# Moving the norm's inverse root from VectorE to Pool in the projections of two layers

## What is computed

```python
def rms_norm_2(x, w):
    xf = x.astype(jnp.float32)
    y = xf * lax.rsqrt(jnp.mean(xf * xf, axis=-1, keepdims=True) + EPS)
    return (y * w.astype(jnp.float32)).astype(x.dtype)

def even_layer(...):                      # layer 2
    proj = rms_norm_2(x, norm_w) @ w_in   # 2048 x 10272
    ...                                   # short convolutions, SSD scan, memory attention, gates
    return x + concat(y_a, y_b, y_m) @ w_out

def odd_layer(...):                       # layer 3
    proj = rms_norm_2(x, norm_w) @ w_in   # 2048 x 3904
    ...                                   # latent attention, memory attention, gates
    return x + concat(y_c, y_m) @ w_out
```

## Time and profile before

| | us |
|---|---|
| median of 3 runs | 1797.61 (1795.02 to 1800.67) |
| the profiled execution | 1793.41 |
| its span in the trace | 1791.2 |
| TensorE busy | 1742.6 (97%) |
| VectorE busy | 1288.3 (72%) |
| ScalarE busy | 899.7 (50%) |
| Pool busy | 125.9 (7%) |

### The profile page before, as it was taken

How to read it: one execution, slowest core, us unless ns; L and a number is a source line. 1 busy time by engine, 2 the same in 40 slices (tenths; PEclk the granted TensorE clock), 3 DMA queues, 4 the chain that set the end, 5 groups by cost and what they waited for, 6 DMA issues and landing times.

```text
span 1791.2 us, 24344 instructions
## 1 busy us (share of the span) xinstructions
PE 1742.6 (97%) x9671; PEld 1496.0 (84%) x9671; DVE 1288.3 (72%) x1622; ACT 899.7 (50%) x1161; POOL 125.9 (7%) x151
## 2 busy tenths in 40 slices
PE   7989999999999999999999999899999999999997
PEld 6778888877888888888888888788888888888885
DVE  6889979785677756887676777965554766778644
ACT  6444443444466445665444556654444545566532
POOL 3321101000010100110000000000000000000000
PEclk9989999999999999999999999999999999999998
DMA  9979979774445566666544555555565564444552
GB/s 359 385 270 349 343 233 326 230 237 136 146 147 175 188 177 188 189 186 178 165 142 141 155 162 166 167 188 188 188 184 176 161 204 141 141 130 131 176 187 96
DMA packets 310400, 350.70 MB, mean 196 GB/s; under 512 B 11296, under 2 KB 284832, under 8 KB 310288
## 3 DMA queue, kind: packets, MB, share of 16 engines
q1 hardware_dynamic: 295728, 296.24, 53.8%
q0 software_dynamic: 14560, 52.89, 8.2%
HBM read 347.00 MB, written 2.10 MB: 195 GB/s over the span
## 4 chain that ended last, share of the span: by engine, by line
PE 67%; DVE 18%; ACT 6%; issue 5%; DMA 2%; SPq 0%; ACTq 0%; DVEq 0%
PE psG L492 37%; PE psG L493 19%; DVE w_lo L422 6%; ACT w_hi L418 3%; DMA raw<-in_mem_w 2%; PE psG L486 2%; PE psG L488 2%; PE psG L487 2%; DVE ada_sum L1260 1%; DVE P L1218 1%; DVE P L1213 1%; PE psH L1876 1%; DMA ada_ring<-in_w_ada 1%; PE psH L1862 1%; DVE gate_sum L1260 1%
## 5 line engine op out<-in xcount | busy, mean ns | idle before, releaser
L492 PE MATMUL psG<-xA,w_hi 128*128 128x512 f32 x2624 | 942.2, 402 | 4.2 <-DVE w_lo L422 3.7
L422 DVE TENSOR_TENSOR w_lo<-raw,w_hi 128x1024 fp32r<-128x1024 f32 (+1 forms) x560 | 688.5, 1240 | 245.5 <-ACT w_hi L418 244.0
L493 PE MATMUL psG<-xA,w_lo 128*128 128x256 f32 x2624 | 734.5, 280 | 0.0
L418 ACT ACTIVATE w_hi<-raw 128x1024 fp32r<-128x1024 f32 (+1 forms) x560 | 570.4, 1043 | 234.9 <-PE psG L493 167.3
L492 PEld LDWEIGHTS psG<-xA,w_hi 128*128 128x128 f32 x2624 | 492.4, 188 | 123.1 <-issue 10.5
L493 PEld LDWEIGHTS psG<-xA,w_lo 128*128 128x128 f32 x2624 | 495.5, 189 | 4.2 <-issue 3.4
L492 PE MATMUL psG<-yP,w_hi 128*128 128x512 f32 x960 | 337.2, 396 | 3.1 <-DVE P L1218 1.6
L493 PE MATMUL psG<-yP,w_lo 128*128 128x256 f32 x960 | 267.9, 279 | 0.0
L492 PEld LDWEIGHTS psG<-yP,w_hi 128*128 128x128 f32 x960 | 180.0, 187 | 45.9 <-DVE P L1218 1.9
L461 ACT ACTIVATE P<-psG 128x512 f32<-128x512 f32 (+2 forms) x103 | 60.9, 592 | 241.3 <-PE psG L493 241.0
L493 PEld LDWEIGHTS psG<-yP,w_lo 128*128 128x128 f32 x960 | 181.0, 189 | 0.2
(11 more groups left out here) (325 smaller groups left out, 1789.9 us busy)
## 6 DMA issues: line engine op xcount, KB each, us to landing
raw<-in_w_in SPq DMA_DIRECT2D x360, 512.0 KB, 3.8
raw<-in_w_out SPq DMA_DIRECT2D x128, 512.0 KB, 3.4
ada_ring<-in_w_ada POOLq DMA_DIRECT2D x96, 512.0 KB, 6.3
raw<-in_mem_w SPq DMA_DIRECT2D x32, 512.0 KB, 10.1
raw<-in_w_uq SPq DMA_DIRECT2D x24, 384.0 KB, 3.3
raw<-in_w_ukv SPq DMA_DIRECT2D x32, 128.0 KB, 2.4
raw<-in_w_ukv SPq DMA_DIRECT2D x16, 256.0 KB, 3.3
P<-in_memT SPq DMA_DIRECT2D x4, 512.0 KB, 7.1
```

What stands on the lines that cost most here:

```text
L418: nc.scalar.activation(high(n), low(n, raw), ACT.Copy).then_inc(hi_ready, 1)
L422: nc.vector.tensor_tensor(low(n), low(n, raw), high(n), ALU.subtract).then_inc(lo_ready, 1)
L492: nc.tensor.matmul(psG[:, bank + f, :], hi[:, w], x, start=first, stop=False)
L493: last = nc.tensor.matmul(psG[:, bank + f, S:2 * S], lo[:, w], x[:, 0:S], start=False, stop=end)
```

## The change

For every copied product of layers 2 and 3 except the one with a bias (G_DT), VectorE stops after the addition and signals `added`. Pool waits for it, multiplies the same tile by the same root in place, and signals `pool_landed`, for which the users of those blocks now wait. 58 blocks are moved: X0, SZ0, SZ1, M, CZ, CV, CC, CB with four each and X1 with eight; C1, M1 with four each, C2 and KR with one each and the two ZC with eight together. Pool takes them in program order; beside the convolution steps it takes one block before each L629 and one after it. Three of the semaphores of the G_DT step are merged into one to make room, with the same order of waits.

```diff
+        self.by_pool = self.copied and norm in (2, 3) and bias is None
...
         def landed(eng, g, blocks=None):
-            eng.wait_ge(scalar_landed if g.by_scalar else vector_landed,
+            eng.wait_ge(scalar_landed if g.by_scalar else pool_landed if g.by_pool else vector_landed,
                         g.landed0 + (g.blocks if blocks is None else blocks))
...
+            def times_root(g, blocks):
+
+                pool.wait_ge(*((q["nm_rs"], 5) if g in G_ZC else (q["nm_rs"], g.norm + 1)))
+                root = (moved_root if g in G_ZC else norm_root_of(g.norm))[0:g.rows].unsqueeze(1).broadcast_to([g.rows, g.parts, S])
+                for b in blocks:
+                    out = g.dst(b)
+                    pool.wait_ge(added, g.landed0 + b + 1)
+                    nc.gpsimd.tensor_tensor(out, out, root, ALU.mult).then_inc(pool_landed, 1)
...
             add_squares(2)
+            times_root(G_X0, range(4))
             for i in range(6):
+                beside, first = (G_X1, 2 * i) if i < 4 else (G_SZ0, 2 * i - 8)
+                times_root(beside, [first])
                 pool.wait_ge(q["cv_s"], i + 1)
                 nc.gpsimd.tensor_tensor(tiles(i * 4 + XS, 4), tiles(CONV_ACC, 4), tiles(CONV_E, 4), ALU.mult)\
                   .then_inc(q["cv_done"], 1)
+                times_root(beside, [first + 1])
+            for g in (G_SZ1, G_M, G_CZ, G_CV, G_CC, G_CB):
+                times_root(g, range(4))
             landed(pool, G_CB)
...
+            for g in (G_C1, G_C2, G_KR, G_M1, *G_ZC):
+                times_root(g, range(g.blocks))
             add_squares(4)
...
                     ins = v.tensor_tensor(out, product(g, b, 1), out, ALU.add)
+                    if g.by_pool:
+                        ins.then_inc(added, 1)
+                        return
                     if g.norm is not None:
```

## The result

| | before | after |
|---|---|---|
| median, us | 1798.24 (1792.65 to 1803.14, 10 runs) | 1811.7 (1805.37 to 1820.96, 10 runs) |
| the profiled execution | 1793.41 | 1812.53 |
| span in the trace | 1791.2 | 1810.7 |

The ratio is 1.0084, with a 95% interval of 1.0063 to 1.0105: the change makes the kernel 0.84% slower, 13.5 us between the medians. The forecast was 1807.9 us within 1799 to 1815. In the changed kernel the high and low matmuls are L495 and L496, the splits L421 (ScalarE) and L425 (VectorE), the copy L464, the addition L1233, Pool's product L611, and the mask product of the SSD step L1576 with its matmul L2086.

A forecast was written before the change was run, and what follows sets the result against it. TensorE, busy for nearly all of 640 to 1663 us, was taken as the bound. Terms of +4.7 + 4.0 + 1.4 + 0.4 + 0.1 - 0.5 + 0.2 = +10.3 gave 1803.7 us profiled, 1807.9 median, range 1799 to 1815.

The forecast's parts named there:

- The mechanism: Behind additions, a Pool product and a VectorE instruction with two SBUF inputs exclude each other; split 2.2 instead of 1.22 us.
- SSD scan: G_M, G_CZ: Pool first at both additions of each of four steps, 2 x 0.58 us fully exposed: +4.7 us.
- "nearly the same" rival: Order turns in the SSD scan only, VectorE first: -1.3 instead of +4.7, total +4.3, 1801.9 us; chance 0.18.
- Convolution: G_X1, G_SZ0: VectorE's already slower loop loses 0.92 us more per step: +4.0 us, bounds 0 and 6.
- G_DT wait: TensorE's 0.9 us wait behind the convolution steps, without any lead, sees 4 x 0.92 = 3.7 us.
- G_M1 to G_UQ: G_UQ's second block: VectorE's split likely first, Pool ends 1.1 us after it: +1.4 us; 0.6 with Pool first.
- The paired starts: G_X0 and G_C1: a block must land within one chunk of 2.77 us, needing about 2.8: +0.4 us for both.
- G_CB and the start of G_OUT0: Up to 0.9 us gained on late low parts, lost again; last block 0.6 later: +0.1 us, between -3 and +3.
- "worse" rival: Back-to-back two-input VectorE instructions make Pool lose in six to ten cases at 1.2 us: 1817 us; chance 0.11.
- Latent attention: PSUM copies after additions start 0.72 us earlier, but blocked splits in G_ZC cost +0.2 us.
- The end: End of the latent attention: earlier PSUM copy removes the 0.5 us wait, gate chain moves with it: -0.5 us.

The follow-up runs named there:

- kernel with the sliver: Changed kernel with Pool's product cut to one column of each 256, all waits and signals kept: 1790.56 us, ratio 0.9957 to the kernel before.
- SSD blocks late on Pool: Changed kernel, but for G_SZ1, G_M and G_CZ Pool starts only after VectorE's split following the addition; also called SSD late: 1814.54 us, ratio 1.0082.
- kernel with its ends back: Changed kernel with the first and last groups G_X0, G_CB, G_C1 and G_M1 (16 blocks) back on VectorE: 1805.82 us, ratio 1.0045.
- SSD back: Changed kernel with G_SZ1, G_M and G_CZ (12 blocks) back on VectorE: 1808.66 us, ratio 1.0053.
- G_CB alone: Changed kernel with only G_CB (4 blocks) on Pool, all else on VectorE: 1803.94 us, ratio 1.0027.
- convolution back: Changed kernel with G_X0, G_X1 and G_SZ0 (16 blocks) back on VectorE: 1815.32 us, ratio 1.0084.
- the twenty such blocks: Changed kernel with only G_SZ1, G_M, G_CZ (started after the next split), G_CV and G_CC on Pool: 1797.59 us, ratio 0.9989.
- G_X0 alone: Changed kernel with only G_X0 (4 blocks) on Pool, all else on VectorE: 1799.72 us, ratio 1.0002.

## Why the prediction was right, step by step

**The mechanism** was the one named: the earlier trace rows showed the exclusion in layer 1, and the changed kernel shows it behind its additions, 2.27 us for a split of 1.22. The kernel with the sliver shows that the detour by itself costs next to nothing, and the SSD blocks late on Pool show the lock apart from Pool's duration: the products there take their full 1.30 us and land later still, and the scan's loss is gone (shift +0.42 instead of +4.93).

**SSD scan**, forecast +4.7: the waits grew from 1.3 to 6.1 us, +4.8, and the shift of the stretch is +4.9. Pool was first, as read from a lead of 0.15 us in the earlier trace rows; the lead was 0.11, since Pool started 0.15 us after the addition's end instead of 0.09. Each of the four steps waits 1.49 to 1.57 us. The "nearly the same" rival, where this order turns, is out.

**Convolution**, forecast +4.0 within 0 to 6: measured +4.75, and +0.04 with those blocks on VectorE. The form was right too: VectorE's loop is the pace-maker. Visible waits in this stretch are only 1.7 us more than before in after, but 3.0 us more in the kernel with its ends back, and the shift is the same 4.8 in both. In after, TensorE ran all 41 undisturbed chunks at its slower pace, and in the other 26 of 40 at the fast one; where TensorE is slower, it waits less. Whoever adds up waits alone undercounts such a loop. The G_DT wait, said to grow to 3.7 us, grew to 1.2 only; the trace had fallen 4.0 us behind ahead of it.

**G_M1 to G_UQ**, forecast +1.4 with VectorE first: 1.42, with VectorE first by 0.04 us. **The paired starts**, forecast +0.4: shifts of 0.27 and 0.38, 0.65 together.

**G_CB and the start of G_OUT0**, forecast +0.1 within -3 to +3: this is one of the two terms that were mis-sized. The waits there are 0.37, 1.57, 1.13, 1.21 and 3.16 us, 7.4 against 5.7 before, +1.7; the hoped-for 0.9 us of relief for the late low parts didn't come. The last block was priced at 0.6 us for landing later, as if Pool were first. The high part of the next chunk was already waiting there, VectorE went on 0.08 us before its addition was even finished, and Pool paid 0.9 us more. The prediction had this case in general words, as its "worse" rival; it should have read the rows at this one place, since it was the block with no slack at all. In the two variants where five VectorE instructions in a row went ahead of Pool, the wait at this place was 7.6 and 7.7 us.

**Latent attention**, forecast +0.2 for blocked splits in G_ZC: this is the other one. From 1605 to 1658 us of before the changed kernel falls 1.1 us behind (1.05 to 1.17 in the seven traces with the full product of G_ZC on Pool), and not at all where G_ZC is on VectorE or Pool's product is a sliver (-0.05 to +0.10). It happens ahead of four matmuls (L1874), by 0.17, 0.20, 0.50 and 0.14 us; the view of the waits lists only the third, as a wait for VectorE's copy from PSUM (L1776). The copy right behind an addition does come 0.7 us earlier, as the prediction said. But the split behind it stands still (2.19 to 2.26 instead of 1.22 us, after each of the three blocks that end in this stretch), and the next copy then comes late: 7.65 us after the first one where the kernel before has 6.67.

```profile
1649.74 0.41 DVE L1776 COPY P<-psH 128x256 f32<-128x256 f32 x1
1650.07 2.20 DVE L425 TENSOR_TENSOR w_lo<-raw,w_hi 128x1024 fp32r<-128x1024 f32 x1
...
1657.39 0.41 DVE L1776 COPY P<-psH 128x256 f32<-128x256 f32 x1
```

**The end**, forecast -0.5: about +0.1. The copy from PSUM moved up as said, but TensorE's wait of 0.59 stayed and Pool's landing made another of 0.41.

**The sum.** By waits the forecast of +10.3 met +10.1, which is partly luck: the convolution and the latent attention show only a part of their loss there. By shifts it is 4.75 + 4.93 + 1.42 + 0.65 + 1.2 for G_CB and the start of G_OUT0 + 1.1 for the latent attention + 0.1 = some 14.1 us, and the medians say 13.5. The slower pace of TensorE in G_OUT0 (1.7 us in the first trace of after, 0.2 in that of SSD back) is left out as the execution's own. The two profiled executions lie 19.1 us apart, because the traces differ by 3.9 us already at 640 us, in layer 1, where nothing was changed; other traces have -0.8 to +7.3 us there.

**Still open** is what decides how long Pool stands when VectorE is first. At G_CB's end it was 2.18 us in four traces (after twice, SSD back, G_CB alone) and 6.71 in two (SSD late, convolution back), with the same instructions at that place and starts that agree within 0.01 us up to the point where the two go apart. Whether one kernel's executions differ in this wasn't seen; the changed kernel's times spread over 15.6 us and those of before over 10.5.

## What to carry to other kernels

Before moving a product from VectorE to Pool, look in the trace at what VectorE does in the 1.3 us behind it. If that is an instruction with two inputs in SBUF, the move trades 0.7 us of VectorE for a lock of 1.3. Where VectorE's own loop is the pace-maker this costs, though the destination has a whole block of slack, as in the convolution. Where a PSUM read or idle time lies there it costs nothing; that it gains anything is not shown by a time here: the twenty such blocks gave a ratio of 0.9989 (0.9972 to 1.0006).

A block whose user is already waiting must not end on the engine that can be kept out. Judge the effect by how far a stretch falls behind, stage by stage, and not by busy times, which count blocked instructions as work, nor by one pair of profiled spans.

## What the runs showed of the hardware that was not expected

**A product on Pool can stand through several VectorE instructions.** In two traces five two-input instructions issued without a pause kept Pool out for 5.4 us (6.71 - 1.27), and it was let in ahead of the sixth; in four others it was let in ahead of the second. The prediction's worse case had priced Pool's losing at 1.2 us a time.

**TensorE has two paces at one granted clock.** A chunk of sixteen matmuls (eight of 512 columns, eight of 256) takes either 2.77 or 2.83 us, for whole stretches without a change. The same code in both traces, first before, then after, every second matmul with the high weights in G_X0, granted clock 1.00:

```profile
700.03 0.39 PE L492 MATMUL psG<-xA,w_hi 128*128 128x512 f32 x1
...
700.72 0.39 PE L492 MATMUL psG<-xA,w_hi 128*128 128x512 f32 x1
```

```profile
704.88 0.40 PE L495 MATMUL psG<-xA,w_hi 128*128 128x512 f32 x1
...
705.59 0.40 PE L495 MATMUL psG<-xA,w_hi 128*128 128x512 f32 x1
```

One starts every 0.346 us, the other every 0.353. Counting the chunks of a whole trace that start 2.80 to 2.86 us before the next, the kernel before had 125 slow ones in one trace and 204 in the other, the changed one 189 and 260, the one with the sliver 143. A difference of 79 chunks by 0.054 us is 4.3 us, so single traces tell these kernels apart only to about 5 us. The pace changed nearly always where TensorE was held or the order of its work was broken. At the late third block of G_X0 it changed in all six traces that have one, from fast to slow in four and from slow to fast in two (SSD late, G_X0 alone), and there in none of the other eight. A like late block in G_C1 changed it in four traces and left it slow in two. So a late landing is a place where the pace can change, but no run showed what selects it.
